# One weight load of a mixture-of-experts decoder step, split into three transfers

## What is computed

```python
for e in range(N_EXPERTS):                      # 32
    a = x @ w1[e] + b1[e]                       # w1[e]: 1024 x 2048
    glu = jnp.minimum(a[:, ::2], SWIGLU_LIMIT)
    lin = jnp.clip(a[:, 1::2], -SWIGLU_LIMIT, SWIGLU_LIMIT)
    act = glu * jax.nn.sigmoid(SWIGLU_ALPHA * glu) * (lin + 1)
    out = out + combine[:, e:e + 1] * (act @ w2[e] + b2[e])   # w2[e]: 1024 x 1024
```

## Time and profile before

| | us, unless marked |
|---|---|
| median of 3 runs | 1113.3 |
| lowest, highest | 1112.66, 1114.51 |
| profiled execution, its own time | 1113.01 |
| profiled execution, span from first to last instruction | 1111.3 |
| TensorE busy in the span | 1055.4 |
| DMA traffic in the span | 431.94 MB, mean 389 GB/s |

### The profile page before, as it was taken

The page is one execution under the profiler, slowest core; times in us unless marked ns, Lnnn a source line. Parts: engine busy times, 40 slices in busy tenths (PEclk is TensorE's granted clock), DMA queues, the critical chain, the costliest instruction groups (busy, mean ns, idle before and its releaser), DMA issues.

```text
span 1111.3 us, 12046 instructions
## 1 busy us (share of the span) xinstructions
PE 1055.4 (95%) x5212; PEld 466.3 (42%) x5212; DVE 259.6 (23%) x522; ACT 171.5 (15%) x412; POOL 24.8 (2%) x63
## 2 busy tenths in 40 slices
PE   7999999999999999999999999899999899999996
PEld 6767855343434334343333324243434343433332
DVE  5645534221111212020201012121212020202122
ACT  3562004120101011110110102020101010101102
POOL 3000012000000000000000000000000000000000
PEclk9999999999999999999999999999999999999999
DMA  9942379999999999999999999999999999999994
GB/s 305 357 173 76 152 275 399 402 426 429 426 428 428 427 427 427 428 428 428 426 427 430 426 428 428 426 429 428 428 428 428 428 426 428 426 428 429 425 421 165
DMA packets 50873, 431.94 MB, mean 389 GB/s; under 512 B 5238, under 2 KB 16190, under 8 KB 25120
## 3 DMA queue, kind: packets, MB, share of 16 engines
q1 hardware_dynamic: 48800, 428.54, 92.6%
q0 software_dynamic: 608, 2.04, 0.6%
q10 hardware_dynamic: 1408, 0.54, 0.2%
HBM read 427.63 MB, written 3.48 MB: 388 GB/s over the span
## 4 chain that ended last, share of the span: by engine, by line
PE 61%; DMA 36%; DVE 1%; issue 1%; ACT 0%; SPq 0%; DVEq 0%
DMA ring<-in_expert_w 35%; PE ps L1883 28%; PE ps L1938 8%; PE ps L1500 7%; PE ps L1805 3%; PE ps L1478 3%; PE ps L1779 2%; PE ps L1626 2%; PE ps L1568 1%; PE ps L1789 1%; PE ps L1720 1%; DMA ring<-in_x_prompt 1%; PE ps L1858 0%; PE ps L1807 0%; PE ps L1712 0%
## 5 line engine op out<-in xcount | busy, mean ns | idle before, releaser
L1883 PE MATMUL ps<-ring,mem 128*64 128x512 f32 x2048 | 464.4, 602 | 16.0 <-DMA ring<-in_expert_w 16.0
L1883 PEld LDWEIGHTS ps<-ring,mem 128*64 128x64 f32 x2048 | 146.3, 138 | 301.8 <-issue 300.7
L1938 PE MATMUL ps<-ring,mem 128*64 128x512 f32 x1024 | 223.9, 594 | 4.4 <-ACT mem L850 3.7
L1301 DVE TENSOR_TENSOR mem<-mem,ps 128x1024 f32<-128x1024 f32 x30 | 36.6, 1221 | 448.3 <-PE ps L1805 414.5
L1938 PEld LDWEIGHTS ps<-ring,mem 128*64 128x64 f32 x1024 | 72.7, 137 | 143.9 <-issue 136.4
L1500 PE MATMUL ps<-ring 128*128 128x266 f32 (+1 forms) x320 | 77.4, 399 | 1.5 <-DVE ring L970 1.5
L855 ACT ACTIVATE mem<-ps 128x264 f32<-128x264 f32 x16 | 6.3, 391 | 446.9 <-PE ps L1858 446.9
L1779 PEld LDWEIGHTS ps<-mem 128*128 128x128 f32 x600 | 65.4, 173 | 13.4 <-issue 12.2
L1779 PE MATMUL ps<-mem 128*128 128x128 f32 x600 | 70.1, 276 | 0.0
L1500 PEld LDWEIGHTS ps<-ring 128*128 128x128 f32 x320 | 60.8, 194 | 16.0 <-issue 4.7
L1805 PE MATMUL ps<-mem 128*128 128x512 f32 x120 | 60.0, 620 | 0.0
(11 more groups left out here) (292 smaller groups left out, 537.5 us busy)
## 6 DMA issues: line engine op xcount, KB each, us to landing
ring<-in_expert_w SPq DMA_DIRECT2D x182, 2048.0 KB, 39.7
ring<-in_expert_w SPq DMA_DIRECT2D x18, 1024.0 KB, 27.9
ring<-in_w_in SPq DMA_DIRECT2D x6, 2048.0 KB, 21.9
ring<-in_w_out SPq DMA_DIRECT2D x2, 2048.0 KB, 11.4
ring<-in_w_in SPq DMA_DIRECT2D x2, 1024.0 KB, 8.5
ring<-in_state_rec SPq DMA_DIRECT2D x4, 512.0 KB, 10.8
out<-ring SPq DMA_DIRECT2D x4, 512.0 KB, 12.9
ring<-in_expert_w SPq DMA_DIRECT2D x4, 512.0 KB, 22.9
```

The source lines that it names most:

```text
L1301: dve.tensor_tensor(h3[:, m], h3[:, m], ps[:, 4 + 2 * m:6 + 2 * m, :].rearrange("p a n -> p (a n)"), ALU.add)\
L1883: done = mm(ps[CAP * e:CAP * e + CAP, b, :], xgT3[:, t, CAP * e:CAP * e + CAP], ring[:, slot[e], col:col + HALF], start=False, stop=(t == ...
L1938: done = mm(ps[CAP * e:CAP * e + CAP, 4 + half, :], actT3[:, 4 * v + t, CAP * e:CAP * e + CAP], ring[:, slot[e], col:col + HALF], start=(v ...
```

## The change

Load 96 alone is issued as three transfers in place of one: its first half for all 128 partitions, and its second half once for partitions 0 to 119 and once for partitions 120 to 127. All three count on the same semaphore, so the count for that place is 32 higher from load 96 on. No other load and no computation is touched.

```diff
+        IN_ROWS = 8 * LOADS
+        ROW_PARTS = (slice(0, 120), slice(120, P))
...
         def first_count(g):

             split = any(g0 <= g and (g - g0) % SLOTS == 0 for g0 in SPLIT_FIRST)
-            return 16 * (g // SLOTS + 1) + (16 if split else 0)
+            parts = IN_ROWS <= g and (g - IN_ROWS) % SLOTS == 0
+            return 16 * (g // SLOTS + 1) + (16 if split else 0) + (16 * len(ROW_PARTS) if parts else 0)
...
+            def load_rows(g, half, rows, signal):
+                p, j = g // LOADS, g % LOADS
+                sp.dma_start(ring[rows, place_of(g), 2048 * half:2048 * half + 2048],
+                             w1_v[2 * p + j % 2, j // 2, rows, half]).then_inc(signal, 16)
...
                 for g in range(SLOTS + 4, in_pieces):
                     sp.wait_ge(w_used, g - SLOTS + 1)
-                    load(g)
+                    if g == IN_ROWS:
+                        load_half(g, 0, ring_in[place_of(g)])
+                        for rows in ROW_PARTS:
+                            load_rows(g, 1, rows, ring_in[place_of(g)])
+                    else:
+                        load(g)
```

## The result

| us, unless marked | before | after |
|---|---|---|
| median of 7 runs each, measured together | 1114.12 | 1116.77 |
| lowest, highest | 1112.66, 1116.45 | 1115.32, 1118.43 |
| profiled execution, its own time | 1113.01 | 1116.70 |
| its span | 1111.3 | 1114.9 |

The ratio is 1.0035, with a 95% interval of 1.0025 to 1.0046: 3.9 us slower, between 2.8 and 5.1. The forecast was 3.3 us slower. The two medians are only 2.65 us apart, and the two profiled executions 3.7, so the size is known to about one us; the expectations of the experiments take the 2.65.

The account below looks back on a forecast made before the run. The sixteen DMA engines' full queues were taken to bound the kernel. 0.1 (packets) + 0.3 (extra row) + 2.0 + 0.9 (collisions) = 3.3 us, on 1113.3, gave 1116.6 us; range 1113.2 to 1118.8.

Parts of the forecast that it names:

- Engines: Load 96's second half: 120 rows on 15 engines, eight each; the other 8 rows on eight engines, one each.
- The rivals with eight engines: 120 rows over eight engines: the late ones, 1115.9 or 1119.4 us, chance 0.08; the early ones, 1110.8 us, chance 0.04.
- Collisions at the places written: Load 96's second half: engines writing where others write hold each other up; 2.9 us, chance 0.58 on 15 engines.
- no collisions: Rival: 120 rows dealt clear of each other, or 32-row packets slow through their source; 1113.7 us, chance 0.30.
- upper bound: Collisions in load 96's second half at most: two engines at half speed each for all 17 rows, 5.3 us.
- the row of equal size: Three transfers of 32 rows each (L626), packets of 8 KB: 0.53 us each, 0.217 above the 0.313.
- the first term: Load 96's second half: nine rows of an engine in foreign places, 9 x 0.217 = 2.0 us.
- The second term: An engine's own ordinary rows hit by others' foreign rows: 0 to 1.7 us, half taken, 0.9 us.
- Extra row, packets: Load 96: one more row on eight engines, 0.3 us; two 8 KB packets per 16 KB packet, 0.1 us.
- Issues: Load 96's three issues for one: 0.80 us at most, covered by 8.8 us before load 97; counted 0.
- Handed on: From load 96 on, queues run in order, so its delay reaches every later load and the end.
- The signs named ahead: Around 620 to 631 us: five-us GB/s dip, full DMA share, slow 8 KB packets, wait longer by two or three us.

Follow-up runs that it names:

- e12: Kernel before, with load 96's second half loaded only for rows 0 to 119, the last eight rows left out: 1117.37 us, ratio 1.0040.
- e1: Kernel before, with load 96 as two halves of 128 rows each, no split by rows: 1113.35 us, ratio 1.0001.
- e2: Kernel before, with load 96 in halves and the second half cut into 112 and 16 rows: 1119.46 us, ratio 1.0053.
- e5: Kernel before, with load 96 in halves and the second half cut into 64 and 64 rows: 1117.93 us, ratio 1.0039.
- e7: Kernel before, load 96's second half as four transfers of eight rows four partitions apart, plus one of 96 rows: 1116.62 us, ratio 1.0035.
- e10: Kernel before, load 96's second half as four eight-row transfers writing neighbouring partitions from rows four apart, plus 96 rows: 1119.84 us, ratio 1.0063.
- e9: Kernel before, load 96's second half as four eight-row transfers writing partitions four apart from neighbouring rows, plus 96 rows: 1117.79 us, ratio 1.0046.
- e3: Kernel before, with the same split by 120 and 8 rows at load 24 in place of load 96: 1116.74 us, ratio 1.0032.

## Why the prediction was right

**Engines: right.** 15 and 8, by the marks of the changed kernel and of e12. The rivals with eight engines needed a power of two and fall with it.

**Collisions at the places written: right.** e1 takes away the split by rows and with it the whole cost. e2 and e5 keep it with sixteen engines and have the cost. e7 to e10 move the place and the source apart for pieces of eight rows, and the slow packets go with the place; for the 120 rows, the main part of the cost by e12, that is concluded from them and not shown by itself. The rival "no collisions" rested on the thought that the slow 32-row packets came from their source; e9 and e10 speak against that as a general cause.

**Its size: too small.** The prediction had 2.0 + 0.9 us for it. The loss in the queue is 4.3 us by the bytes that were missing, nearer to its upper bound of 5.3. By the packets' records, engines lost about 2.8 us each on 8 KB packets and 1.8 us on 16 KB packets. 180 of the 256 packets of 8 KB took more than 0.4 us, 0.56 on average, 0.25 above the 0.313; the row of equal size had 0.53. If the 128 of the second half are all among them (the records do not name the row), they make 8 x 0.25 = 2.0 us an engine, the first term, and the other 52, of the first half, make 0.8, near the 0.9. The second term is the one that was mis-sized all the same: an engine's ordinary rows were counted as the eight of load 96 alone. What was hit were 16 KB rows as well, of the loads before and behind, since the engines stand at different points of the queue (the marks of load 96 land 3.9 us apart in the kernel before); between 620 and 628 us these took 1.05 to 1.15 us on average in place of 0.617, and their 1.8 us were not in the sum. In that stretch packets of both sizes took 1.7 to 1.9 times as long as undisturbed ones (0.55 to 0.58 against 0.313). The prediction's upper bound had two engines at half speed each; that factor of two was the author's estimate, and no run shows two engines at one place. The measured 1.7 to 1.9 stand in its place.

**Extra row, packets: too small to see.** 0.3 and 0.1 us were counted. e1 shows no cost for the packets and the issue (1.0001); the eight-row piece with its extra row is worth 0.1 to 0.7 us of landings (e12).

**Issues: hidden, but barely.** I priced two more issues at 0.80 us, against 8.8 us of cover, and counted 0. SyncE's issues of load 96's three transfers, then of 97 and those behind it, in the kernel after:

```profile
579.32 2.74 SPq L470 DMA_DIRECT2D ring<-in_expert_w  x1
582.11 8.55 SPq L462 DMA_DIRECT2D ring<-in_expert_w  x2
590.84 13.57 SPq L456 DMA_DIRECT2D ring<-in_expert_w  x4
```

They took 11.3 us, up to 590.66, and load 97 was due at 590.82. The cover was used up almost to the last tenth, and the price of 0.80 us was wrong. No cost came of it: in e7, too, the issues of the second half, five of them, take 8.52 us and end just ahead of load 97's, and e7's ratio is that of the change. In e1 one issue took 4.24 us and the time did not change, and in e3 all three took 1.2 us and the cost was there. The queue had work all the while: loads 96 and 97 landed 40 us and more after their issue.

**Handed on: right.** In the kernel before, loads 96, 97, 98 and the next landed at 625.6, 631.3, 636.3 and 641.2 us, in the order of their issue. In the kernel after, load 97 was 4.5 us late, the last load's first half 4.45, the last vector step 4.46; e3 shows the same over three quarters of the run. "Nothing later has slack" holds up to the output's stores, which were 0.85 us shorter in this execution.

**The signs named ahead.** The dip, the full share, the slow packets and the longer wait came. The dip lasted eleven us and not five, and the wait grew by 4.3 us and not two or three: both follow from the one term. The sum, 3.3 us, was near the measured 3.9 partly by luck: the queue lost a us more than that, and the stores gave nearly as much back. That the forecast of 1116.6 us is so close to the median of 1116.77 is luck as well: it was built on 1113.3 for the kernel before, which took 1114.12 in these runs.

## What to carry to other kernels

In this kernel a load cut into transfers to all 128 partitions kept its rate (e1: 428 GB/s, ratio 1.0001); one cut by partitions into blocks did not, even when it was cut evenly (e5: 231 GB/s, ratio 1.0039), and in the full queue it slowed its neighbours too (after: packets of 16 KB took 1.05 to 1.15 us in place of 0.617). Cut a load along its row (columns, as in e1) when it must be cut. A full DMA share says that engines are busy, not that they move bytes (after: a share of 1.03 at 244 GB/s): look for the dip in GB/s beside it, and turn the missing bytes into us at the usual rate.

## What the hardware showed that I had not expected

The price of one split grows along the run: 4.0, then 4.5 to 5.4, then 6 to 7.5 us by the landings at loads 24, 96 and 132. By the times it is 3.6, 3.9 and 6.0 us, with intervals that overlap. A reason that was only argued: the sixteen marks of a load land 2.3, 3.9 and 5.4 us apart at these three loads in the kernel before, and 7.0 from 890 us on, so the foreign rows meet other engines' packets for longer. Load 24 has a shorter queue ahead of it as well: it lands 19 us after its issue, load 96 after 45.8. What drives the engines apart was not tried.

An issue took some 4.3 us where two in a row took 0.80 before: each of the two pieces of the second half took that long in the kernel after, somewhat less than the 4.9 us in which the queue moves one load (2.1 MB at 428 GB/s). In e7 the five pieces together took the same 8.5 us (one of them 4.28, the others 0.6 to 1.2), so it is not a price of each issue. It came with nine or ten loads outstanding, by the 45.8 us to the landing at 4.9 us a load; at load 24, which lands 19 us after its issue, the three issues took 1.2 us in all. Whether the depth of the queue is what makes an issue slow was not tried.

How 120 rows are dealt out over fifteen engines, which engines are late at the end, and whether a deal by hand of all 128 rows into pieces, each row written by the engine that writes it in a whole load, would be free, stays open.
